# A first stage by token tiles, a bias table copied inside DRAM, and six changed hand-overs in a one-core transformer layer

## The reference

```
h = rmsnorm(x, norm_mix_pre)
(a_q, a_kc, a_vc, a_ks, a_vs, a_kw, a_vw, a_g,
 b_q, b_k, b_v, b_r, b_lr, c_q, c_k, c_v, mg) = split(h @ w_in)
o_a = nsa_mixer(a_q, ..., gates=a_g, rel_a)
o_b = gla_mixer(b_q, b_k, b_v, log_sigmoid(b_lr @ w2 + b) / 16, b_r)
o_c = moba_mixer(c_q, c_k, c_v, rel_c)
merged = sum over branches of sigmoid(mg_i) * (o_i @ w_branch_i)
x = x + rmsnorm(merged @ w_out)
x = x + rmsnorm((silu(gate) * up) @ w_ffn_out)
```

## Time and profile before

| what | value |
|---|---|
| median of 3 runs | 983.66 us (982.23, 983.66, 986.11) |
| the profiled execution | 981.99 us |
| its span, first to last instruction | 980.2 us |
| mean granted TensorE clock | 0.992 of full |
| PE busy | 945.7 us |
| DVE, ACT, POOL busy | 467.2, 404.6, 195.2 us |

### The profile page before, as it was taken

The page is one execution under the profiler, slowest core; times in us unless marked ns, Lnnn a source line. Parts: engine busy times, 40 slices in busy tenths (PEclk is TensorE's granted clock), DMA queues, the critical chain, the costliest instruction groups (busy, mean ns, idle before and its releaser), DMA issues.

```text
span 980.2 us, 13035 instructions
## 1 busy us (share of the span) xinstructions
PE 945.7 (96%) x4708; PEld 793.4 (81%) x4708; DVE 467.2 (48%) x874; ACT 404.6 (41%) x726; POOL 195.2 (20%) x183
## 2 busy tenths in 40 slices
PE   5999999999999999999989998999999999999996
PEld 4888888888788888888878787988888888888884
DVE  6377563362455556555567657223232323333335
ACT  4443353343456666667645344222222222323233
POOL 4442353333124324344310001000000000000000
PEclk9999999999999999999999999999999999999999
DMA  6278136312232232364275451022323222323222
GB/s 229 88 104 182 47 100 201 108 65 88 85 108 84 89 108 81 119 243 129 77 289 194 160 172 54 33 86 86 106 89 103 89 103 89 103 86 107 86 86 87
DMA packets 38030, 111.39 MB, mean 114 GB/s; under 512 B 4117, under 2 KB 8661, under 8 KB 37469
## 3 DMA queue, kind: packets, MB, share of 16 engines
q1 hardware_dynamic: 37692, 110.23, 35.2%
q10 hardware_dynamic: 288, 0.52, 0.2%
HBM read 93.93 MB, written 13.66 MB: 110 GB/s over the span
## 4 chain that ended last, share of the span: by engine, by line
PE 89%; DMA 4%; DVE 3%; ACT 2%; issue 1%; DVEq 0%; POOL 0%; SPq 0%; ACTq 0%
PE bank L1596 26%; PE bank L1598 25%; PE bank L1597 25%; DMA w_raw<-wpack 3%; PE bank L656 3%; PE bank L673 2%; PE bank L648 2%; PE bank L671 1%; PE bank L647 1%; ACT w_hi L911 1%; DMA gl_in<-gate_logits 1%; PE bank L1632 1%; DMA xs<-x_in 1%; PE bank L1612 1%; DVE x L1572 0%
## 5 line engine op out<-in xcount | busy, mean ns | idle before, releaser
L1596 PE MATMUL bank<-h_hi,w_lo 128*128 128x512 f32 (+1 forms) x680 | 269.8, 397 | 1.4 <-DVE h_lo L1178 1.4
L1597 PE MATMUL bank<-h_lo,w_hi 128*128 128x512 f32 (+1 forms) x680 | 265.8, 391 | 0.0
L1598 PE MATMUL bank<-h_hi,w_hi 128*128 128x512 f32 (+1 forms) x680 | 265.7, 391 | 0.0
L911 ACT ACTIVATE w_hi<-w_raw 128x1024 fp32r<-128x1024 f32 (+1 forms) x89 | 93.6, 1052 | 165.5 <-PE bank L1598 157.2
L1596 PEld LDWEIGHTS bank<-h_hi,w_lo 128*128 128x128 f32 (+1 forms) x680 | 127.6, 188 | 28.8 <-issue 3.5
L1598 PEld LDWEIGHTS bank<-h_hi,w_hi 128*128 128x128 f32 (+1 forms) x680 | 127.7, 188 | 28.2
L1597 PEld LDWEIGHTS bank<-h_lo,w_hi 128*128 128x128 f32 (+1 forms) x680 | 127.9, 188 | 23.6
L845 POOL TENSOR_TENSOR w_lo<-w_raw,w_hi 128x1024 fp32r<-128x1024 f32 (+1 forms) x37 | 88.4, 2390 | 136.7 <-ACT w_hi L911 136.6
L1099 ACT ACTIVATE w_hi<-w_raw 128x1024 fp32r<-128x1024 f32 x36 | 38.2, 1061 | 152.3 <-PE bank L1598 152.3
L852 POOL TENSOR_TENSOR sc<-sc,ast 128x512 f32<-128x512 f32 (+1 forms) x96 | 66.2, 721 | 136.4 <-DVE ast L562 103.0
L1185 DVE TENSOR_TENSOR w_lo<-w_raw,w_hi 128x1024 fp32r<-128x1024 f32 x52 | 64.2, 1235 | 51.5 <-ACT w_hi L911 51.2
(11 more groups left out here) (280 smaller groups left out, 1544.1 us busy)
## 6 DMA issues: line engine op xcount, KB each, us to landing
w_raw<-wpack SPq DMA_DIRECT2D x146, 512.0 KB, 3.3
gate_logits<-gl_out SPq DMA_DIRECT2D x24, 256.0 KB, 2.2
gl_in<-gate_logits SPq DMA_DIRECT2D x24, 256.0 KB, 3.7
near_bias<-near SPq DMA_DIRECT2D x1, 3072.0 KB, 33.1
xs<-x_in SPq DMA_DIRECT2D x4, 512.0 KB, 5.6
fullb<-near_bias SPq DMA_DIRECT2D x16, 128.0 KB, 2.8
ckx<-cks SPq DMA_DIRECT2D x16, 128.0 KB, 2.7
ob<-gla_out SPq DMA_DIRECT2D x2, 1024.0 KB, 6.0
```

What stands on the lines that cost most here:

```text
L911: sa.activation(split_weights(c)[0][:, 0:n], raw[:, s, 0:n], ACT.Copy).then_inc(w_hi, 1)
L1596: mm(out, ll, rh, start=start, stop=False, skip_group_check=True)
L1597: mm(out, lh, rl, start=False, stop=False, skip_group_check=True)
L1598: return mm(out, lh, rh, start=False, stop=stop, skip_group_check=True)
```

## The change

- **First stage.** `agl` and `nv` are replaced by three chunks `nx`, which hold for 3, 3 and 2 blocks of 128 rows of `w_in` the 296 columns `a_vs`, `a_vw`, `b_lr`, `a_g`. The tokens are on the partitions of the result: 96 matmuls of 296 columns. They are interleaved by hand with the transposes of the four token tiles. The norm's weight is now loaded as a full 128 x 1024 tile (`wpre`, 512 KB, the second transfer of the kernel) and multiplied in `x_scale`; input tiles are split per token tile and half. The low parts of the first four chunks move from POOL to DVE, and chunks 2 and 3 get slots of their own. Only the 16 low-rank columns are transposed. The weight loads are spread among those of x.
- **The near table.** ACT's queue writes 8 copies of each head's row, and later a second transfer copies that block of 12 KB in DRAM 15 times per head.
- **Six hand-overs.** Attention's first maximum goes ahead of the low part of the last key chunk, and the next weight split behind the second maximum; the bias fill goes earlier. The compressed step waits one chunk later. The loads of `xr` and the two norm rows go behind the logits, one per pair of products. The output projection waits for 22 products at its first chunk and for 24 at its second. `transposed_lo(1)` goes ahead of the third tile's norm. The last two down chunks get slots of their own.

```diff
-STRAIGHT = ([("agl", 0), ("bq", 0), ("bq", 1), ("bk", 0), ("bk", 1)]
+STRAIGHT = ([("nx", j) for j in range(3)] + [("bq", 0), ("bq", 1), ("bk", 0), ("bk", 1)]
...
-            + [("nv", 0), ("nv", 1), ("aq", 2), ("aq", 3)]
+            + [("aq", 2), ("aq", 3)]
...
+NX_K, NX_W = ((0, 1, 2), (3, 4, 5), (6, 7)), 2 * P + 40
...
+            elif c in (N_CHUNKS - 2, N_CHUNKS - 1):
+                eng.wait_ge(w_used, C_FIN + 4)
...
+                    if u == 0:
+                        stacked_low(C_MERGE - 1)
+                    if u == 1:
+                        lo(C_GATE + 1)
...
+            load_x(0)
+            sp.dma_start(wpre[:, :], rows_d[3, :, :]).then_inc(pre_in, 16)
+            for t in range(1, NT):
+                load_x(t)
+                fetch(t - 1)
...
-                if c == 10:
-                    sp.wait_ge(near_ready, 18)
-                    sp.dma_start(near_dram, near[64:80, :].unsqueeze(1).broadcast_to([16, P, D_NEAR])).then_inc(near_out, 16)
...
+                if c == NEAR_AT:
+                    sa.wait_ge(near_ready, 18)
+                    sa.dma_start(near_dram[:, 0:8, :],
+                                 near[64:80, :].unsqueeze(1).broadcast_to([16, 8, D_NEAR])).then_inc(near_first, 16)
+                if c == NEAR_AT + 3:
+                    sa.wait_ge(near_first, 16)
+                    sa.dma_start(near_dram[:, 8:P, :].rearrange("h (a b) d -> h a (b d)", b=8),
+                                 near_dram[:, 0:8, :].rearrange("h (a b) d -> h a (b d)", b=8)
+                                 .broadcast_to([16, P // 8 - 1, 8 * D_NEAR])).then_inc(near_out, 16)
...
-            sp.dma_start(xr[:, :, :], x_d.rearrange("(t p) d -> p t d", p=P)).then_inc(xr_in, 16)
-            sp.dma_start(wpost[:, :], rows_d[0, :, :]).then_inc(posts_in, 16)
-            sp.dma_start(wfpre[:, :], rows_d[1, :, :]).then_inc(posts_in, 16)
...
+                if 4 <= j < 4 + NT:
+                    t = j - 4
+                    sp.dma_start(xr[:, t, :], x_d[t * P:(t + 1) * P, :]).then_inc(xr_in, 16)
+                elif 4 + NT <= j < 6 + NT:
+                    row = j - 4 - NT
+                    sp.dma_start((wpost, wfpre)[row][:, :], rows_d[row, :, :]).then_inc(posts_in, 16)
...
-                ve.tensor_scalar(xs[:, t, :], xs[:, t, :], stat[:, 4 + t:5 + t], None, ALU.mult).then_inc(xn_ready, 1)
+                ve.scalar_tensor_tensor(out=xs[:, t, :], in0=xs[:, t, :], scalar=stat[:, 4 + t:5 + t],
+                                        in1=wpre[:, :], op0=ALU.mult, op1=ALU.mult).then_inc(xn_ready, 1)
...
+            x_sum(0)
+            x_average(0)
+            ve.wait_ge(pre_in, 16)
+            x_scale(0)
+            x_average(1)
+            x_scale(1)
+            input_lo(0)
+            x_average(2)
+            lo(0)
+            x_scale(2)
+            input_lo(1)
+            lo(1)
+            x_average(3)
+            x_scale(3)
+            input_lo(2)
+            lo(2)
+            input_lo(3)
+            lo(3)
...
-                else:
-                    transposed_lo(ve, t - 2)
+                elif t == 2:
+                    transposed_lo(ve, 0)
+                    transposed_lo(ve, 1)
...
+            input_transposes(0)
+            input_transposes(1)
+            early(0, 0, ("both", "h_lo"))
+            early(1, 0, ("both",))
+            early(0, 0, ("w_lo",))
+            input_transposes(2)
...
+            input_transposes(3)
+            early(0, 2, ("both", "h_lo"))
+            early(1, 2, ("both", "h_lo"))
...
-                if c == C_O + 5:
+                if c == C_O + 6:
...
-                    if m == 0 and t == 2:
-                        te.wait_ge(d_free, N_GATES)
+                    if m < 2 and t == 2:
+                        te.wait_ge(d_free, N_GATES - 2 + 2 * m)
```

More of the change, by code:

```diff
@@ L232, in program @@
         extra = {}
-        for name, first, kib in (("out", C_OUT + 4, 72), ("gate0", C_FIN, 168), ("gate1", C_FIN + 2, 184)):
+        for name, first, kib in (("start", 2, 72), ("out", C_OUT + 4, 72), ("gate0", C_FIN, 168), ("gate1", C_FIN + 2, 184),
+                                 ("last", N_CHUNKS - 2, 168)):
             pair_hi = at(kib, f"wx_{name}_hi", [P, 2, CHUNK], F32R)
@@ L1598, in three, with feature_major @@
                 return mm(out, lh, rh, start=False, stop=stop, skip_group_check=True)
[L1600 to L1605 removed]
+            def feature_major(out, c, ks=range(KD)):
+                high, low = split_weights(c)
+                for k in ks:
+                    cols = slice(k * P, k * P + P)
+                    last = three(out, high[:, cols], low[:, cols], hh[:, k, :], hl[:, k, :], k == 0, k == KD - 1)
+                return last
@@ new lines, in input_transposes @@
+            def input_transposes(t):
+                te.wait_ge(xn_ready, t + 1)
+                for half in range(2):
+                    if t >= 2:
+                        te.wait_ge(h_lo, 2 * (t - 2) + half + 1)
+                    for k in range(4):
+                        last = te.transpose(input_bank(t, half)[:, k * P:k * P + P],
+                                            xs[:, t, (4 * half + k) * P:(4 * half + k) * P + P], ident[:, :])
+                    last.then_inc(xT_full, 1)
@@ new lines, in early @@
+            def early(t, j, parts):
+                high, low = split_weights(j)
+                te.wait_ge(w_hi, j + 1)
+                if "w_lo" in parts:
+                    lo_split(te, j)
+                halves = 2 * t + NX_K[j][-1] // 4 + 1
+                te.wait_ge(h_lo if "h_lo" in parts else h_hi, halves)
+                for part in parts:
+                    x, weights = {"both": (hh, high), "h_lo": (hl, high), "w_lo": (hh, low)}[part]
+                    for i, k in enumerate(NX_K[j]):
+                        cols = slice(i * NX_W, i * NX_W + NX_W)
+                        last = mm(bank[t][:, 0:NX_W], x[:, k, t * P:t * P + P], weights[:, cols],
+                                  start=part == "both" and k == 0, stop=part == "w_lo" and k == KD - 1,
+                                  skip_group_check=True)
@@ L1616, in aux_free_for @@
+            for t in range(3):
+                early(t, 2, ("w_lo",)).then_inc(tm_done, 1)
+            for j in range(3):
+                early(3, j, ("both",))
+            for j in range(3):
+                early(3, j, ("h_lo",))
+            for j in range(3):
+                last = early(3, j, ("w_lo",))
+            last.then_inc(w_used, 3)
             def aux_free_for(name):
```

349 lines of the change are left out of this document (185 added, 164 removed).

## The result

The changed kernel took **952.39 us** (median; 952.27 to 953.53), the kernel before, on the same chip in turn, 982.94 (981.71 to 986.11). The ratio is 0.9687, 95% interval 0.9662 to 0.9712. The profiled span fell from 980.2 to 950.6 us, by 29.6. Forecast were 957.6 and 26.1 us of gain: the direction was right and the waits that were to go went, the size was too small, and the measured median lies 0.1 us under the low end of the range.

What follows compares the result with a forecast made beforehand. PE was taken to bound the kernel, by matmul work and idle seams. First stage 3.9, near table 1.5, hand-overs 15.9 and clock 4.8 sum to 26.1 us: span 954.1, median 957.6 us, range 952.5 to 967.5.

Steps and rivals of the forecast that it cites:

- What bounds it: Whole kernel: PE busy 945.7 of 980.2 us, so only less matmul work or less of its 34.5 us idle helps.
- First stage: Start of the kernel: 3.9 us gained, `bq` starting 7.6 us later against 11.5 saved later; bounds 1.2 and 6.3.
- The layout by hand: First stage: step-by-step timing of DVE and PE, last `x_scale` at 19.6 us, `bq` at about 28.7, taken as 29.3.
- Near table: PE's wait at `qblock`, with weights late behind the 3 MB transfer: the whole 1.5 us gained; lower bound 0.
- Six hand-overs: Seams between stages: six PE waits removed, 1.5, 2.1, 2.7, 1.9, 4.7 and 3.0 us, in sum 15.9 us.
- The two seams with 0.4 and 0.6 us of room: Logits (gain 2.7, room 0.4 us) and residual loop (gain 4.7, room 0.6): inputs expected ready just before PE asks.
- rival 1: Hand-overs: the next wait takes the place, costing half of 15.9 us and one slow stretch: 967 us; chance 0.17.
- rival 5: Hand-overs: the change does not do what it says, all six void: 978 us; chance 0.03.
- Clock: Slow PE clock after the waits at 508, 558 and 607 us: 4.8 us expected to go with those waits.
- Rival 2: Clock: the waits go but the slow clock stays, price 4.8 us: 962.4 us; chance 0.12.
- the best start: First stage: PE never waits after 8.64 us and ends at 26.9, a gain of 6.3, 2.4 us above the forecast.
- the clock's bound: Slow clock: gain between nothing, if a slow stretch comes elsewhere, and 4.8 us.

Runs made afterwards that it cites:

- the fourth further execution: The kernel before, unchanged, profiled again: 992.23 us, span 990.5, of which 15.4 us lost to the clock.

## Why the prediction was right in kind and too small

**What bounds it** was right: PE's work and PE's seams. Nothing else appeared.

**First stage: 3.9, measured 4.5 by milestones and 4.9 by undoing it.** The layout by hand gave 28.7 for `bq`; I then took 29.3 "for the hand-overs", and the row reads 28.65. That added 0.6 is the error of this term. The price of the 296-column matmul was right within 0.001 us, those of DVE's steps within 0.15 (two low parts 1.28, not 1.41).

**Near table: 1.5, measured 1.7 in this trace,** and 1.1 to 1.4 as a difference of spans when put back. The size holds for this execution only: in five executions of the kernel before this wait was 0.3 to 4.4 us. The mechanism was half right: the transfer behind which the weights stood did cost PE, and its move took the wait away, but the faster copy, which was half of the reason given, does nothing for PE, and queue and moment were not told apart.

**Six hand-overs: 15.9, measured 16.9 in milestones without the clock** (distances of starts: 1.6, 2.3, 2.9, 2.0, 4.9, 3.2). Each removed wait was worth 0.1 to 0.2 us more than its row. The list of waits counts idle time from the modelled end of the last matmul, while what a removed wait gives back is the distance of two starts less the usual 0.23 us. The two seams with 0.4 and 0.6 us of room held, with no wait in the rows: rival 1 did not happen, nor rival 5.

**Clock: 4.8, measured 6.9 less about 0.4 in idle time. This is the step that failed,** and it failed in two places. First, I read the windows around the listed waits only. The windows at 190 to 200 us, with no wait beside them, lose another 1.7 us, which the forecast put at nothing. Second, I set the median 1.7 us above the profiled execution in the new kernel too, because it lay there in the old one; it came out 0.1 above (952.39 against 952.27). Of the 5.2 us between 957.6 and 952.4 these two make 3.3. Rival 2 (the clock stays slow) did not happen: at the hand-overs the slow stretches went with the waits.

Luck is in this term on both sides. This execution of the kernel before lost only 6.9 us, others 8.6 to 15.4. The stretch near 193 us stood in four of five executions of it and, near 185 us, in six of fourteen profiles of the changed kernel and its variants, but not in the one compared here: of its 1.7 us about 0.6 can be expected to last (my estimate, 1.7 x (4/5 - 6/14)). The gain of the medians was 30.5 us in the first set of runs, 33.0 in the second (985.72 to 952.69) and 36.4 in the last (990.12 to 953.68).

**The sum.** The four corrections are 0.6 to 1.0 (first stage), 0.2, 1.0 and 1.7: 26.1 + 3.5 to 3.9 = 29.6 to 30.0, against 29.6 in the spans. The gain of 30.5 in the medians has another 0.8 from the changed kernel's median lying 0.1 above its profiled execution, where the old one's lay 0.95 above (982.94 against 981.99). Without the clock the spans are 973.3 and 950.6: 22.7 us of the gain are work and waits, for which the forecast had 21.3.

**The range.** Below the forecast it held only the best start (2.4) and the spread (2), which reach down to 953.2; the 952.5 that stands there has another 0.7 us without a reason. Every hand-over was capped at its own row, so nothing could come out larger, and the clock's bound ended at the stretches that I had named. A bound of the clock taken over all windows of the trace (6.9 for 4.8) would have been 2.1 us lower and would have held the result.

## What to carry to other kernels

Sum the loss of clock over all windows of the trace, not only beside the waits, and treat it as different in each execution: profile the kernel before more than once. Price a removed wait by the distance of starts around it less the usual one, not by the idle time of the list. A long transfer ahead of weights in their queue went with a wait of 0.3 us in one execution and 4.4 in the next, so its row in one trace does not price it; moved to another queue and a later moment it cost nothing in any of the profiles.

## What the runs showed of the hardware

- The granted clock fell to 1.2 GHz (a window of 0.50, matmuls of 512 columns 0.43 us apart instead of 0.23) behind waits of 1.5 to 4.7 us and also behind a busy stretch of 32 matmuls of 64 columns, and at one and the same place it did so in one execution and not in the next. One fall cost 1.7 us in most rows (0.66 in one window), and up to 3.4 us (0.50 and 0.83 in two windows of the fourth further execution, 0.60 and 0.72 with the low part of tile 1 put back).
- Times of the kernel before go with its mean clock: 980.69 us at 0.994, 983.8 at 0.992, 987.0 to 990.9 at 0.987, 992.5 at 0.984. With the waits went most of the spread: 951.9 to 954.2 in twelve further runs of the changed kernel.
- A copy inside DRAM of 2880 KB in runs of 12 KB took 14.0 us, some 210 GB/s; 3 MB from on-chip memory in runs of 1.5 KB took 33 to 35 us, on SP's queue at 52 to 59 us and on ACT's at 84.
- Four chunks of weights of 512 KB on SP's queue landed in 14.5 us in the median beside the transfer of 3 MB in runs of 1.5 KB on ACT's queue, and in 3.3 beside the two-step copy.
- Three copies inside DRAM in a row made the weights of the other queue land in 11.4 instead of 3.3 us: two queues share what lies behind them.
- Two executions of the kernel before differed by up to 8.5 us in what the clock took (6.9 and 15.4). Nothing in the first trace told of it; what decides it in one execution is open.
